# Four more gathered rows asked for early, and eight dot products ahead of the groups

## The reference

```python
q = (xt @ w_query).reshape(T, N_RET_HEADS, 2, HALF_KEY)
s = jnp.einsum('thpd,hpnd->thpn', q, sub_keys)
s_half, i_half = lax.top_k(s, TOPK_HALF)          # 16 of 128 keys, twice a head
cand_s = s_half[:, :, 0, :, None] + s_half[:, :, 1, None, :]
top_s, pos = lax.top_k(cand_s, TOPK)              # 16 of 256 pairs a head
ids, gates = take(cand_i, pos), softmax(top_s)
a = gelu(einsum('chkd,cd->chk', u_tab[ids], x))   # one dot product per expert
y = einsum('chk,chkd->cd', gates * a, v_tab[ids])
```

## Time and profile before

| | us |
|---|---|
| median of 3 runs | 3485.97 |
| lowest and highest | 3479.86, 3488.27 |
| the profiled execution | 3496.24 |
| its span | 3494.4 |

### The profile page before, as it was taken

The page is one execution under the profiler, slowest core; times in us unless marked ns, Lnnn a source line. Parts: engine busy times, 40 slices in busy tenths (PEclk is TensorE's granted clock), DMA queues, the critical chain, the costliest instruction groups (busy, mean ns, idle before and its releaser), DMA issues.

```text
span 3494.4 us, 63120 instructions
## 1 busy us (share of the span) xinstructions
PE 3328.6 (95%) x19278; PEld 2443.3 (70%) x19278; DVE 2984.3 (85%) x6039; ACT 2191.8 (63%) x3118; POOL 1330.3 (38%) x1126
## 2 busy tenths in 40 slices
PE   6999999999999999999989999999999998999999
PEld 5767775667777667767777677666677776676776
DVE  6899777998888778888869997789988886888888
ACT  3574435567777666777746724455677776766776
POOL 0000017316555556557500000271265564555554
PEclk9999999999999999999999999999999999999999
DMA  5312272459999999999923123535699999999998
GB/s 199 103 61 69 89 264 97 156 190 326 363 354 331 319 353 345 363 350 359 339 81 90 61 79 121 211 115 179 221 335 361 345 341 310 360 355 351 344 361 296
DMA packets 421669, 868.89 MB, mean 249 GB/s; under 512 B 167824, under 2 KB 233360, under 8 KB 421008
## 3 DMA queue, kind: packets, MB, share of 16 engines
q1 hardware_dynamic: 310512, 544.87, 46.3%
q0 software_dynamic: 73728, 268.47, 21.3%
q10 hardware_dynamic: 37152, 52.45, 4.1%
HBM read 774.41 MB, written 85.98 MB: 246 GB/s over the span
## 4 chain that ended last, share of the span: by engine, by line
PE 40%; issue 26%; DVE 15%; POOL 10%; DMA 4%; ACT 3%; DVEq 0%; POOLq 0%; SPq 0%; ACTq 0%
PE ps L924 9%; PE ps L927 8%; PE ps L928 8%; POOL gbuf L586 6%; POOL spare L600 5%; PE ps L636 4%; PE ps L638 3%; PE ps L637 3%; DVE yT L1506 3%; DVE i L1752 2%; DMA raw<-stream 2%; DVE v L1748 1%; DVE S_ring L1758 1%; DMA gbuf<-u_rows,ids_u 1%; PE ps L670 1%
## 5 line engine op out<-in xcount | busy, mean ns | idle before, releaser
L670 PE MATMUL ps<-h,w 128*128 128x384 f16 (+1 forms) x2272 | 760.0, 335 | 40.1 <-ACT w L1012 40.0
L671 PE MATMUL ps<-h,w 128*128 128x384 f16 (+1 forms) x2272 | 756.8, 334 | 0.0
L1012 ACT ACTIVATE w<-w_hi 128x1024 f16<-128x1024 f32 x544 | 572.5, 1052 | 286.3 <-DVE w L1934 174.5
L600 POOL TENSOR_TENSOR spare<-spare 128x1 f32<-128x1 f32 x504 | 393.9, 782 | 909.2 <-DVE a_sp L1740 500.9
L927 PE MATMUL ps<-cf,w 128*128 128x384 f16 x2032 | 665.2, 328 | 0.0
L928 PE MATMUL ps<-cf,w 128*128 128x384 f16 x2032 | 662.2, 327 | 0.0
L667 PE MATMUL ps<-h_hi,w_hi 128*128 128x384 f32 (+1 forms) x2272 | 489.9, 357 | 0.0
L924 PE MATMUL ps<-cf_hi,w_hi 128*128 128x384 f32 x2032 | 430.6, 354 | 23.6 <-DVE cf L1928 23.6
L1934 DVE SCALAR_TENSOR_TENSOR w<-raw,w_hi 128x1024 f16<-128x1024 f32 x256 | 313.3, 1224 | 132.8 <-ACT w_hi L1007 113.6
L667 PEld LDWEIGHTS ps<-h_hi,w_hi 128*128 128x128 f32 x2272 | 396.0, 189 | 17.4 <-issue 0.3
L1000 ACT ACTIVATE w_hi<-raw 128x1024 fp32r<-128x1024 f32 x296 | 313.7, 1060 | 144.6 <-DMA raw<-stream 105.5
(11 more groups left out here) (286 smaller groups left out, 6241.7 us busy)
## 6 DMA issues: line engine op xcount, KB each, us to landing
raw<-stream SPq DMA_DIRECT2D x682, 512.0 KB, 5.6
gelu_scratch<-g_out ACTq DMA_DIRECT2D x256, 192.0 KB, 6.0
cg<-gelu_scratch SPq DMA_DIRECT2D x256, 192.0 KB, 6.8
c_scratch<-stage SPq DMA_DIRECT2D x128, 256.0 KB
cg<-c_scratch SPq DMA_DIRECT2D x256, 128.0 KB, 5.7
qT<-ada SPq DMA_DIRECT2D x32, 512.0 KB, 6.2
cgate<-ada SPq DMA_DIRECT2D x32, 512.0 KB, 5.4
w_rows<-ada SPq DMA_DIRECT2D x32, 512.0 KB, 6.4
```

Source lines behind the costliest of these rows:

```text
L600: nc.gpsimd.tensor_tensor(spare[:, 16:17], spare[:, 17:18], spare[:, 18:19], ALU.add).then_inc(room, 1)
L670: nc.tensor.matmul(ps[:, b, 0:n], w16[:, s, 0, c], h16[:, c, 1, t0:T], start=False, stop=False)
L671: mm = nc.tensor.matmul(ps[:, b, 0:n], w16[:, s, 1, c], h16[:, c, 0, t0:T], start=False, stop=c == C - 1)
L1012: nc.scalar.mul(w16[:, s, 1], w_hi[:, s].bitcast(F32), X_DOWN).then_inc(w16_done, 1)
```

## The change

GpSimd asks for rows 0 to 7 as soon as the row numbers are known. Rows 4 to 7 go to a new buffer, `early_rows`, four slots of 4 KB a partition that lie where the one-hots of the groups are written later; rows 0 to 3 and all from 8 on go to `gbuf` as before. The four new slots have semaphores of their own. Gathers from 8 on wait as before. VectorE does eight dots ahead of the groups, with a low part after the second and after the sixth, and 110 dots over the groups.

```diff
-DOTS_FIRST, DOTS_BY_GROUP = 4, 114
+DOTS_FIRST, DOTS_BY_GROUP = 8, 110
+        early_rows = at("early_rows", base + 74 * KB, [P, SLOTS, D])
+        early_in = [sem(f"early_in{s}") for s in range(SLOTS)]
...
                     nc.gpsimd.indirect_dma_start(
-                        out=gbuf[:, n % SLOTS], out_offset=None, in_=table,
-                        in_offset=bass.IndirectOffsetOnAxis(ap=ids[:, k:k + 1], axis=0)).then_inc(row_in[n % SLOTS], 16)
+                        out=early_rows[:, n % SLOTS] if SLOTS <= n < 2 * SLOTS else gbuf[:, n % SLOTS], out_offset=None, in_=table,
+                        in_offset=bass.IndirectOffsetOnAxis(ap=ids[:, k:k + 1], axis=0)).then_inc(
+                            early_in[n % SLOTS] if SLOTS <= n < 2 * SLOTS else row_in[n % SLOTS], 16)
...
-                for n in range(SLOTS):
+                for n in range(2 * SLOTS):
                     gather(n)
-                for n in range(SLOTS, 2 * P):
-                    pool.wait_ge(room, l * (2 * P - SLOTS) + n - SLOTS + 1)
+                for n in range(2 * SLOTS, 2 * P):
+                    pool.wait_ge(room, l * (2 * P - 2 * SLOTS) + n - 2 * SLOTS + 1)
                     pool.wait_ge(row_used, l * 2 * P + n + 1)
...
-                    dve.wait_ge(row_in[k], (l * (2 * P // SLOTS) + n // SLOTS + 1) * 16)
-                    row = gbuf[:, k].rearrange("t (c d) -> t c d", c=2 * C)
+                    early = SLOTS <= n < 2 * SLOTS
+                    if early:
+                        dve.wait_ge(early_in[k], (l + 1) * 16)
+                    else:
+                        dve.wait_ge(row_in[k], (l * (2 * P // SLOTS - 1) + n // SLOTS + (n < SLOTS)) * 16)
+                    row = (early_rows if early else gbuf)[:, k].rearrange("t (c d) -> t c d", c=2 * C)
...
                 for n in range(DOTS_FIRST):
                     dot()
-                    if n == 1:
+                    if n in (1, 5):
                         u_low()
```

More of the change, by code:

```diff
@@ L1910, in weigh @@
                     at_k = dve.snap(4 * r + k)
-                    dve.wait_ge(row_in[k % 4], (l * (2 * P // SLOTS) + P // SLOTS + r + k // 4 + 1) * 16)
+                    dve.wait_ge(row_in[k % 4], (l * (2 * P // SLOTS - 1) + P // SLOTS + r + k // 4) * 16)
                     dve.wait_ge(row_used, l * 2 * P + P + 4 * r + k + 4)
```

## The result

The changed kernel takes 3492.65 us (median of 20 executions) and the kernel before 3483.24 us (20 on the same chip): a ratio of 1.0027, 95% interval 1.0017 to 1.0037, so +9.4 us, between +5.9 and +12.9. The time lies inside the range on record, and it is within 0.3%, though the interval reaches over that. But the sum behind it was +2.4 us; the rest of this document is about the other 7 us.

What follows compares the result with a forecast made beforehand. TensorE, busy 95% of the span, was taken as the bound, VectorE in the routing stretch. The terms, 2 x (0.3 + 2.2 - 1.0 - 0.3) = +2.4 us on the median 3485.97 us, gave 3488.4 us; range 3476 to 3498 us.

Steps and rivals of the forecast that it cites:

- The four extra requests: Routing stretch, after the row numbers: four more gathers crowd the DMA and delay a weight tile, +0.3 us a layer.
- the 6.8 us on which the prediction leaned: Landing time of a weight tile among the first four gathers, against 3.4 us shortly before; read as agreeing with the rule.
- Eight dots first: Start of the groups: four more dots delay low(33), TensorE loses 1.6 us at tile 33 and 0.6 at group 1, +2.2 us a layer.
- The rows that follow: Group stretch: the lead stays four rows, so dot 11's stop (3.89 us on VectorE, 1.95 on TensorE) returns at dot 15.
- rival 1: Group stretch: half the row gaps and late-tile gaps go, -6.0 us, 3480 us; sign: row waits under 30 us; chance 0.25.
- Fewer dots per group: Group stretch: 110 dots over 48 groups, not 114, give 14 groups with three dots, not 18; -1.0 us a layer.
- less traffic: Group stretch: 2.1 MB of 147 MB leave it, so a tenth of the late-tile gaps goes, -0.3 us a layer.
- 15.2 us of TensorE over 36 threes: Group stretch: TensorE's gaps after VectorE row stops, spread over groups with three dots, 0.42 us each.
- rival 3: Routing stretch: late weight tiles stop VectorE, 6.1 us a layer, +14 us in all, 3500 us; chance 0.12.
- Rival 2: Start of the groups: the 2.2 us disappear into TensorE's later row wait, -2.0 us in all, 3484 us; chance 0.20.

Runs made afterwards that it cites:

- second trace: The changed kernel run again with no edit, for a second profile: ratio 1.0032 to the kernel before.
- the requests alone: The kernel before with four more gathers a layer behind the first four, into a buffer that nothing reads: ratio 1.0018, +6.3 us.
- four idle dots: The kernel before with four more dots behind the first four, on data at hand, results unused, a low part after the second: ratio 1.0001, +0.3 us.
- the run with narrow pieces: The kernel before with four more gathers of 128 pieces of 1 KB behind the first four, values unused: first dot 88.8 / 88.8 us, one execution.

## Why the prediction was right in the range and wrong in the sum

*The four extra requests*: this is the mis-sized step. +0.3 us a layer was taken, with bounds of 0 and +3.5. Measured at the first dot: 3.5 and 2.5 us in the changed kernel, 3.3 and 1.8 in its second trace, 1.6 and 1.9 for the requests alone; 2.8 us a layer is the mean for the changed kernel. The text had right that VectorE is the bound of this stretch and that GpSimd's own time is hidden. It went wrong in pricing the requests by one thing that VectorE waits for, a weight tile: VectorE stood for its own late count, and between steps, with no weight tile in question. The comparison that covered the term, the low half's start at 695.13 us against ScalarE's end at 694.68 us, was never what mattered.

The rule cited there ("DMA: Bandwidth & Descriptors" of the Trainium skill, "Queues, rings and completion order") says that each DMA engine goes round the queue rows that have work. Between 694 and 698 us of the changed kernel 1.69 MB move, and GpSimd's queue (q0) has 462 of the 466 packets:

```profile
DMA packets 466, 1.69 MB, mean 422 GB/s; under 512 B 54, under 2 KB 54, under 8 KB 466
## 3 DMA queue, kind: packets, MB, share of 16 engines
q0 software_dynamic: 462, 1.69, 103.1%
q10 hardware_dynamic: 3, 0.00, 0.0%
q1 hardware_dynamic: 1, 0.00, 0.0%
```

SyncE asks for a weight tile at 694.79 us, once the late count has come, and ScalarE issues a gelu store at 695.25 us; the tile's first packet starts at 698.21 us, and ScalarE stands 3.97 us for it. The kernel before has the same: a tile asked for at 685.62 us, its first packet at 689.34 us, and only GpSimd's packets in between. So the 6.8 us on which the prediction leaned did not show the rule at work. Whether the other queues were passed over, or their work reached the DMA engines late, no run tells apart.

*Eight dots first*: +2.2 us a layer, right in size and place (1.52 + 0.60 and 1.64 + 0.62 us; 2.5 and 2.4 us from the first dot to group 2). The experiment with four idle dots shows the same gaps.

*The rows that follow*: the stop came back at dot 15 as said, at half the length. Row waits fell to 23.0 us, not to 40 to 48; under 30 us had been named as rival 1's sign. The lead per gather is indeed unchanged, but the stops nevertheless shrank in every kernel with 110 dots over the groups (11 to 14 us a layer in ten layers, against 17 to 26 in eighteen layers with 114); why is not shown. The 50.1 us from which the forecast started was the highest of the nine traces with 114 dots.

*Fewer dots per group* and *less traffic*: -1.3 us a layer was taken; nothing came. TensorE's idle time from group 0 to the last group, summed from the traces, is 9.7 us a layer in the 18 layers with 114 dots (6.7 to 13.1) and 10.4 us in the ten with 110 (7.5 to 13.8), the 0.6 us ahead of group 1 counted where they stand. The step that failed is "15.2 us of TensorE over 36 threes": it charged each gap to the VectorE stop that stood just before it. With shorter stops, the gaps come elsewhere. ScalarE's waits for weight tiles are as long as they were, 45.6 us in layer 0's groups and 32.6 in layer 1's (41.8 and 36.6 before); that these tiles now end the gaps is likely, but not shown:

```profile
ACT w_hi L1003 <- DMA raw<-stream: 45.6, 40, 3.0
```

```profile
ACT w_hi L1003 <- DMA raw<-stream: 32.6, 33, 4.3
```

With what the landmarks of the changed kernel's trace show, the sum is (3.5 + 2.5) + (2.5 + 2.4) + 0 = +10.9 us, against +9.4 (+5.9 to +12.9) timed. *The rivals*: rival 3 has the place and the sign right (VectorE idle for 3.5 us between 690 and 715 us, over the 2 named), by another mechanism and at under half its 6.1 us a layer. Rival 1's sign appeared and its gain did not, so a shorter wait of VectorE was no sign of a gain. Rival 2 is left with at most a part. The predicted 3488.4 us lay 4.3 us under the measured time, less than the sum's 7.0, by luck: it stood on the median of three executions, 3485.97 us, which twenty put at 3483.24. The range held because it was 22 us wide around a sum whose largest term was far too small.

## What to carry to other kernels

Price a burst of gathers by its number of requests as well as its bytes, and look at what the other engines do while it is issued: here spreading the same four gathers over weight tiles removed a loss of 2 to 4 us a layer at the first dot (90.5 and 89.3 to 86.7 and 87.2). A wait that disappears from an engine with 70 us to spare is no gain until the bounding engine's idle time falls over several traces; one trace of after alone (5.4 and 7.8 us ahead of the half-word pass in the two layers, against 10.9 and 11.1) would have claimed a gain that kernels without the change show as well. A gap that a view puts down to "issue" or "remote" can still be a wait: read in the code what stands in front of it, and in the trace when that semaphore rose. And work put ahead of a pipelined stage shows as a gap at its start, even when the same work is taken out later.

## What the runs showed of the hardware

Four gathers of 128 rows, 1.24 us apart, hold nothing up. With six or more in a row (five were not run) semaphore counts that other engines raise arrive late. TensorE's count of finished tiles, 0.01 us behind the end of a tile in the kernel before, comes 3.0 us late with six, 4.3 us in the changed kernel and 9.7 us with twelve (layer 0). ScalarE stands for it: 5.20 us in the changed kernel, 5.03 us in the run with narrow pieces, where TensorE then loses 0.5 us. VectorE stands from 7.3 to 8.2 us after the first request on, by 0.9 us with six and 1.9 to 3.5 with seven or eight; each of its stops of 1.2 us or more up to eight gathers is at a wait for its own count and ends 0.03 us after that count rises. Twelve cost 6.0 to 6.6 us a layer. What holds the counts up is open: no instruction-loading packet falls into VectorE's stops, and what GpSimd, its queue and the semaphores share was not measured separately. That the short stops between steps have the same source is likely, but not shown.
